# Sixteen columns of the second block's modulation moved from the MLP's up halves to two projections

## What is computed

```
mod = silu(c) @ w_ada + b_ada                   # 6 parts of 2048
sh1, sc1, gt1, sh2, sc2, gt2 = split(mod, 6)
h = rmsnorm(x, g_mix) * (1 + sc1) + sh1
x = x + gt1 * mixer(h)                          # ends in y @ w_out
h = rmsnorm(x, g_ffn) * (1 + sc2) + sh2
x = x + gt2 * ffn(h)
out = rmsnorm(x, final_g)
```

```
x = x + g1 * rmsnorm(merged @ w_o)              # the projection in front of the MLP
x = x + g2 * rmsnorm(square(relu(h @ mlp_up)) @ mlp_down)
```

## Time and profile before

| | us |
|---|---|
| median of 3 runs | 3304.55 (3303.95 to 3306.34) |
| the profiled execution | 3306.13 |
| its span, first to last instruction | 3304.4 |
| TensorE busy | 3223.1 |
| VectorE busy | 2204.1 |
| ScalarE busy | 1242.0 |
| GpSimd busy | 196.1 |
| granted TensorE clock, mean | 0.991 |

### The profile page before, as it was taken

The page is one execution under the profiler, slowest core; times in us unless marked ns, Lnnn a source line. Parts: engine busy times, 40 slices in busy tenths (PEclk is TensorE's granted clock), DMA queues, the critical chain, the costliest instruction groups (busy, mean ns, idle before and its releaser), DMA issues.

```text
span 3304.4 us, 58756 instructions
## 1 busy us (share of the span) xinstructions
PE 3223.1 (98%) x23408; PEld 2700.8 (82%) x23408; DVE 2204.1 (67%) x3396; ACT 1242.0 (38%) x1686; POOL 196.1 (6%) x298
## 2 busy tenths in 40 slices
PE   7999999999999999989999999989999999999998
PEld 4764685578888999978888888878888888888887
DVE  2377656665555666667877787787666767667666
ACT  2202130144444411344443444444544443443444
POOL 0000000012222000000000000000000000000000
PEclk9999999999999999999999999999999999999999
DMA  9956727622222688636767777645444557556654
GB/s 409 364 204 229 275 85 262 253 75 91 96 92 85 263 332 346 235 142 253 277 245 268 254 260 257 254 167 180 160 152 178 191 190 264 209 188 243 227 178 153
DMA packets 101013, 709.02 MB, mean 215 GB/s; under 512 B 11200, under 2 KB 11328, under 8 KB 19520
## 3 DMA queue, kind: packets, MB, share of 16 engines
q1 hardware_dynamic: 73872, 525.89, 43.4%
q0 software_dynamic: 23184, 169.88, 13.8%
q10 hardware_dynamic: 3744, 10.23, 0.8%
HBM read 698.36 MB, written 7.60 MB: 214 GB/s over the span
## 4 chain that ended last, share of the span: by engine, by line
PE 91%; DVE 4%; DMA 3%; issue 1%; ACT 1%; DVEq 0%; SPq 0%; POOL 0%; POOLq 0%; ACTq 0%
PE ps L2708 33%; PE ps L2707 17%; PE ps L633 11%; PE ps L2411 3%; PE ps L1100 3%; PE ps L399 2%; PE ps L2704 2%; PE ps L1823 2%; PE ps L1101 2%; PE ps L1102 2%; PE ps L1837 1%; PE ps L1092 1%; PE ps L2705 1%; PE ps L2392 1%; PE ps L2394 1%; PE ps L2393 1%
## 5 line engine op out<-in xcount | busy, mean ns | idle before, releaser
L2708 PE MATMUL ps<-hT_parts,rows_parts 128*128 128x512 f32 x3210 | 1130.2, 394 | 0.0
L2707 PE MATMUL ps<-hT_parts,ring_parts 128*128 128x256 f32 x3210 | 900.8, 281 | 2.1 <-DVE hT_parts L2680 2.1
L2671 DVE TENSOR_TENSOR ring_parts<-ring,rows_parts 128x2048 fp32r<-128x2048 f32 (+1 forms) x337 | 761.8, 2261 | 108.0 <-ACT rows_parts L2666 107.1
L2666 ACT ACTIVATE rows_parts<-ring 128x2048 fp32r<-128x2048 f32 (+1 forms) x337 | 639.3, 1897 | 407.8 <-DMA ring<-in_mlp_u 210.0
L2708 PEld LDWEIGHTS ps<-hT_parts,rows_parts 128*128 128x128 f32 x3210 | 603.0, 188 | 125.8
L2707 PEld LDWEIGHTS ps<-hT_parts,ring_parts 128*128 128x128 f32 x3210 | 607.7, 189 | 12.8 <-DVE hT_parts L2680 3.3
L2708 PE MATMUL ps<-work_parts,rows_parts 128*128 128x512 f32 x1616 | 570.1, 394 | 0.0
L2707 PE MATMUL ps<-work_parts,ring_parts 128*128 128x256 f32 x1616 | 453.7, 281 | 0.0
L633 PE MATMUL ps<-hT,ring 128*128 128x512 f32 (+1 forms) x1088 | 365.6, 498 | 0.0
L2708 PEld LDWEIGHTS ps<-work_parts,rows_parts 128*128 128x128 f32 x1616 | 303.6, 188 | 63.7
L633 PEld LDWEIGHTS ps<-hT,ring 128*128 128x128 f32 x1088 | 206.6, 190 | 157.3 <-issue 145.0
(11 more groups left out here) (495 smaller groups left out, 4481.7 us busy)
## 6 DMA issues: line engine op xcount, KB each, us to landing
ring<-in_mlp_u SPq DMA_DIRECT2D x128, 1024.0 KB, 5.0
ring<-in_ffn_u SPq DMA_DIRECT2D x88, 1024.0 KB, 4.9
rows<-in_mod_r POOLq DMA_DIRECT2D x64, 1024.0 KB, 5.3
ring<-in_gate_u SPq DMA_DIRECT2D x64, 1024.0 KB, 5.3
work<-in_ada_r POOLq DMA_DIRECT2D x64, 1024.0 KB, 5.3
ring<-in_in_u SPq DMA_DIRECT2D x36, 1024.0 KB, 4.9
rows<-in_ada_r POOLq DMA_DIRECT2D x32, 1024.0 KB, 9.3
ring<-in_down_u SPq DMA_DIRECT2D x32, 1024.0 KB, 4.9
```

The source lines that it names most:

```text
L2666: act.activation(unit_high(u)[:, 0:size], slot(u)[:, 0:size], ACT.Copy).then_inc(hi_done, 1)
L2671: dve.tensor_tensor(ring_parts[:, ring_slot(u), 0:size], slot(u)[:, 0:size], unit_high(u)[:, 0:size].bitcast(F32), ALU.subtract)\
L2707: pe.matmul(ps[:, b, low_half], low, top(kt), start=False, stop=False)
L2708: mm = pe.matmul(ps[:, b, :], high, both(kt), start=False, stop=kt == kts - 1)
```

## The change

The 16 columns of the MLP's up halves are taken out. Eight are done in `Mix`, behind units 1 and 3 of each turn of four, and eight in the output projection at the head of `Ffn2`, behind units 0 and 2 of each turn. The order of the columns stays. `Mix` gets a GpSimd part that fetches eight rows once `Merge` has split its sum; `Mlp` fetches 32 instead of 48; `Ffn2` fetches eight once the mixer's output is split, ahead of its waits and clearings. The first `late_free` and `late_done` are given at the start of `Mix` on VectorE. `gffn` moves from the start of `In2` to the last unit of the output projection, where it waits for the last of the 48 columns.

```diff
+        MIX_ROWS = OUT2_ROWS = KT // 2
@@ class Mix
+            def gpsimd(pool, own):
+                pool.wait_ge(x_split, KT)
+                fetch_late(pool, 0, MIX_ROWS)
@@ wo_sum
                             rms_y1.add_square(dve, sq1[:, bass.ds(it * 4 + j, 1), :], j, it * 4, it * 4)
+                        if j % 2:
+                            late_column(dve, it, j // 2, 2)
+                dve.sem_inc(late_free, 1)
+                dve.sem_inc(late_done, 1)
                 rms_y1.clear_sum(dve)
@@ Mlp
-        UP_COLUMNS = (2, 5, 8, 11)
-        MLP_COLUMNS = LATE_ROWS // QUARTERS
+        UP_COLUMNS = ()
+        MLP_ROWS = LATE_ROWS - MIX_ROWS - OUT2_ROWS
+        MLP_COLUMNS = MLP_ROWS // QUARTERS
                 pool.wait_ge(x_split, KT)
-                fetch_late(pool, 0, LATE_ROWS)
+                fetch_late(pool, MIX_ROWS, MLP_ROWS)
                 dve.sem_inc(act_split, 2)
-                dve.sem_inc(late_free, 1)
-                dve.sem_inc(late_done, 1)
-                dve.wait_ge(late_done, LATE_ROWS + 1)
+                dve.wait_ge(late_done, MIX_ROWS + MLP_ROWS + 1)
@@ In2
-                own.step(dve.scalar_tensor_tensor(gffn, adaT[:, 4 * KT:5 * KT], 1.0, vec("g_ffn"), ALU.add, ALU.mult))
@@ Ffn2
             def gpsimd(pool, own):
+                pool.wait_ge(x_split, 4 * KT)
+                fetch_late(pool, MIX_ROWS + MLP_ROWS, OUT2_ROWS)
                 pool.wait_ge(nadd, 3 * KT)
@@ out2_sum
                             rms_x3.add_square(dve, squared[:, j % 2, :], j, it * 4, it * 4)
+                        if j % 2 == 0:
+                            late_column(dve, it, MIX_ROWS + MLP_ROWS + j // 2, 2)
+                        elif last and j == 3:
+                            dve.wait_ge(late_done, LATE_ROWS + 1)
+                            own.step(dve.scalar_tensor_tensor(gffn, adaT[:, 4 * KT:5 * KT], 1.0, vec("g_ffn"), ALU.add, ALU.mult))
+                            own.settle()
```

More of the change, by code:

```diff
@@ L2826, in branch_kernel @@
         use_mlp = [bk.take(b, QUARTERS * MLP_USES) for b in range(MLP_BANKS)]
-        UP_COLUMNS = (2, 5, 8, 11)
-        MLP_COLUMNS = LATE_ROWS // QUARTERS
+        UP_COLUMNS = ()
+        MLP_ROWS = LATE_ROWS - MIX_ROWS - OUT2_ROWS
+        MLP_COLUMNS = MLP_ROWS // QUARTERS
+        assert MLP_COLUMNS == len(UP_COLUMNS) + KT // 2
         act_parts = work_parts[:, 0:2 * KT * T].rearrange("p (a t) -> p a t", a=KT)
@@ L2917, in vector @@
                             if n in UP_COLUMNS:
-                                late_column(dve, q, UP_COLUMNS.index(n), MLP_COLUMNS)
+                                late_column(dve, q, MIX_ROWS + UP_COLUMNS.index(n), MLP_COLUMNS)
                         else:
@@ L2924, in vector @@
                             if n % 2 == 0:
-                                late_column(dve, q, len(UP_COLUMNS) + (n - KT) // 2, MLP_COLUMNS)
+                                late_column(dve, q, MIX_ROWS + len(UP_COLUMNS) + (n - KT) // 2, MLP_COLUMNS)
                     rest_unit(dve, seg_mlp + 2 * KT + AHEAD_DVE, q * (2 * KT))
-                dve.wait_ge(late_done, LATE_ROWS + 1)
+                dve.wait_ge(late_done, MIX_ROWS + MLP_ROWS + 1)
                 rms_y2.vector(dve)
@@ L3762, in _ @@
                 Merge.gpsimd(pool, own)
+                Mix.gpsimd(pool, own)
                 Mlp.gpsimd(pool, own)
```

## The result

The changed kernel takes 3310.05 us (median of 18 runs, 3305.06 to 3315.48) where the kernel before takes 3303.88 us (median of 18, 3298.63 to 3306.34). The ratio is 1.0021, with an interval of 1.0014 to 1.0028: **slower by 6.9 us** (4.6 to 9.3; from the ratio, the two medians alone are 6.2 us apart). In a second measurement of the same two kernels the ratio was 1.0023 (1.0014 to 1.0032). The forecast was 3307.5 us, +3.0, with "no change" as the likeliest case. The time is inside the stated range; the loss is over twice what the prediction's sum gave, and just beyond the 0.2% that was called no change.

The account below looks back on a forecast made before the run. TensorE was taken to bound the kernel, so only seams could change: -2.14 + 1.08 + 2.4 + 1.66 = +3.0 us, added to the median 3304.55 for 3307.5 us. The range was 3303.5 to 3310.5 us.

Parts of the forecast that it names:

- The bound: Whole kernel: TensorE is busy 98% of the span, so freeing VectorE in the up halves gains nothing; only seams change.
- rival 4: Up halves: VectorE or transfers hold them after all, hidden by busy time; faster, 3266 us; chance 0.02.
- Seam 1: Start of the MLP: first row no longer in front of the ring transfers; gain 2.14 us, bounds 0 and 2.5.
- rival 5: Start of the MLP: the fetch does not start early and the gain is missed; 3309.6 us; chance 0.06.
- Seam 2: End of the first projection: eighth column delays the norm's reciprocal; loss +1.08 us, bounds 0.5 and 1.3.
- rival 2: TensorE's lower clock after longer idling in the norms, seams 2 and 4; at most 1.7 us, 3309.2 us; chance 0.10.
- Seam 3: Start of the second projection: first row lands behind the ring transfer, stalling unit 3; +2.4 us, bounds 0 and 3.0.
- Rival 1: Start of the second projection: row gets ahead of the ring transfer, no stall; 3305.1 us; chance 0.12.
- Seam 4: End of the second projection: eighth column behind unit 14 delays unit 15's sum; +1.66 us, bounds 1.2 and 1.8.
- Inside the second projection: Middle of the second projection: a column makes the next sum 1.7 us late, bank wanted 2.6 us later; costs nothing.
- rival 3: Second projection: two banks too few if rows land later than 10.5 us; at 12.5 us, 3321 us; chance 0.04.
- The sum: Four seams together: -2.14 + 1.08 + 2.4 + 1.66 = +3.0 us, giving 3307.5 us.

Follow-up runs that it names:

- e5: The kernel before with the two signals releasing the first row moved ahead of the first projection, no column moved; 3299.47 us, ratio 0.9992.
- e10: The kernel before, unaltered, traced a second time; one run, 3296.88 us.
- e9: The changed kernel with six columns in each projection, behind units 1 and 3, none in the last turn, four back in the up halves; 3303.58 us, ratio 1.0006.
- e6: The kernel before with the up halves' columns behind units 5, 8, 11, 14 instead of 2, 5, 8, 11; 3300.95 us, ratio 0.9998.
- e2: The changed kernel with only the second projection's eight columns; the other eight back in the up halves, ready signals in the MLP's code; 3306.75 us, ratio 1.0022.
- e1: The changed kernel with only the first projection's eight columns; the other eight back in the up halves, scale back at the input projection; 3305.44 us, ratio 1.0010.
- e3: The changed kernel with the first projection's column ahead of the square's addition instead of behind it; 3309.75 us, ratio 1.0025.
- e11: The changed kernel with six columns in each projection, none in the last turn, each ahead of the addition of the squares; 3301.21 us, ratio 0.9997.
- e7: The kernel before with the first row released early and the up halves' columns behind units 5, 8, 11 and 14; 3300.82 us, ratio 0.9997.
- e8: The changed kernel, unaltered, traced and timed once more; 3309.15 us, ratio 1.0023.
- e12: The changed kernel with the first projection's column ahead of the square's addition, measured a second time; 3306.93 us, ratio 1.0009.

## Why the prediction was right or wrong

- **The bound: right.** TensorE loses and gains nothing in the middle of the MLP and of the first projection, and in the second nothing from the second unit behind the stall on. Sixteen columns, 41.6 us of VectorE, left the up halves and bought nothing there (0.00 us between unit 7 and the last product); rival 4 is dead.
- **Seam 1: right, against the trace read.** Forecast -2.14, measured -2.17, by the mechanism named (e5). Against e10 the gain is 1.16. The bounds of 0 and 2.5 held, and rival 5 is dead; the step that failed in part is that one trace was taken for the kernel.
- **Seam 2: wrong, the largest miss.** Forecast +1.08, measured +3.58. The column in the norm was right in place and nearly in size (0.87). The failed step is "Inside this segment a column delays the next sum by about 0.9 us, against a full unit of 5.6 us until the bank is wanted; nothing." It asked only whether TensorE would have to wait for a bank inside the segment. It did not ask whether VectorE makes the delay up before the segment ends. Sums of units 10 to 12 in the kernel after, with a column between the last two:

```profile
1418.81 0.42 DVE L2755 TENSOR_TENSOR work<-work,ps 128x256 f32 x1
1423.83 0.41 DVE L2755 TENSOR_TENSOR work<-work,ps 128x256 f32 x1
...
1430.16 0.41 DVE L2755 TENSOR_TENSOR work<-work,ps 128x256 f32<-128x256 f32 x1
```

A unit without a column takes VectorE's chain 5.02 us (with the waits for ScalarE's square and rounding in it, which are part of the chain), one with a column 6.33: 11.35 us for two units. TensorE needs 2 x 5.59 = 11.18. The chain is 0.17 us too long here (the pairs before this one took 11.26 to 11.98), so it doesn't catch up. VectorE starts behind in the kernel before as well, but at 5.02 against 5.59 it gains 0.57 us a unit, and by its fourth sum it waits for ScalarE again:

```profile
1367.64 0.41 DVE L2754 TENSOR_TENSOR work<-work,ps 128x256 f32 x1
...
1383.41 0.42 DVE L2754 TENSOR_TENSOR work<-work,ps 128x256 f32 x1 [0.49 <-ACT work L2749]
```

  The lag is harmless as long as TensorE runs, and what is left of it, 2.20 us, comes due where TensorE waits for the last sum. It is not all there at the start. In the kernel before a sum that is on time starts 0.84 us behind the start of TensorE's next unit (0.61 us in the last turn). Against that the first sum of after is 1.2 us late (before's is 1.0), the one behind the first column 2.0, since VectorE waited 0.60 us for the first row, and the one at the last turn's start 3.3; the last turn, with a shorter chain, takes 1.1 off. Its rival, the hold in the norm alone, would have left e9 at 0; e9 had 1.44. The busy share of VectorE hid this (56% of the middle of this projection before the change, by the earlier trace rows, and 75% with the columns), since the waits inside the chain count as idle. The other 0.51 us are the clock, which rival 2 had as a possibility.
- **Seam 3: the stall right, what follows it missing.** Forecast +2.4, measured +3.71. The ring went first, the row landed in 7.4 us (forecast about 8.0), and the stall was 2.15 us. By the Trainium skill (DMA: Bandwidth & Descriptors, Anatomy of one DMA, SWDGE path) the row would take 4.4 us alone, an estimate; the traces don't agree: a row alone ahead of the ring took 5.3 us in e6, one beside it 7.4 here. What is missing showed as the unit behind the stall, 1.57 us at a granted clock of 0.76. Rival 2 had the clock, but priced it only at seams 2 and 4, "at most 1.7 us", and not where the change makes a stall of its own. And e2 shows that a clock that stays up would not have saved the forecast: the late row leaves VectorE behind, and 1.41 us of that come due at seam 4 instead. The step that failed is the same as at seam 2, that a late VectorE costs nothing between the seams. Rival 1 is dead: the row never got ahead.
- **Seam 4: right in its term.** The last sum is 1.47 us late, forecast 1.66. The forecast took VectorE to be on time at unit 14; in after it was, within 0.1 us at the column's start, but only behind the slow unit (e2's last sum is 2.88 us late). The stretch's total depends on the clock: it is +0.76 in e10 and +1.47 in e1, neither with a column there, so the +1.72 can't be all put down to the change; against e10 it is +0.96.
- **Inside the second projection: right for TensorE.** TensorE is busy for 56.00 of 56.00 us, and VectorE waits for no row behind the first in a way that reaches TensorE; rival 3 is dead. What the lag does up to the segment's end is told at seam 3.
- **The sum.** The four seams came to 3.58 - 2.17 + 3.71 + 1.72 = +6.84 us instead of +3.0. The misses are +2.50 at seam 2 (2.20 of lag, 0.51 of clock, less 0.21 of hold) and +1.31 at seam 3 (1.57 of clock, less 0.25 of stall). The timed difference is 6.9, but this nearness is partly luck: all stretches of the same two traces give 6.16 us, and against the second trace of before they give 7.2. That the time fell inside the stated range is luck too, since both large losses, at seams 2 and 3, were taken too small.

## What to carry to other kernels

An engine with idle time can still have no room: add up its serial chain over one period of the loop, waits for its neighbours included, and compare it with the period of the bound engine. If it is longer by anything at all, a lag that was made up before now reaches the seam, and each new delay adds to it. Put filler work into a wait that the chain has anyway (e3: ahead of the square's addition) and leave it out of a loop's last turn (e9); e11 did both, and its ratio was 0.9997. Where a change makes one transfer late, the stall is not the whole price: the engine that waited stays behind, and its debt is paid by a slow unit or at the segment's end (5.2 to 6.0 us for seams 3 and 4, where the stall is 2.15). And take a difference of under 0.3% from stretches of two traces of each kernel, not from spans.

The lowest ratio of all versions is e5's, the early row alone, at 0.9992 (0.9983 to 1.0001): not clear of no change. e7 has the same early row and came to 0.9997.

## What the runs showed of the hardware

- **The clock behind a short stall.** TensorE idled 1.98 and 1.86 us in front of one unit of after and e8, and was granted 0.76 over that unit; in e3 and e12 (1.83 and 1.91 us) the unit took 7.1 us too. Behind 1.79 us in e2 the clock stayed at 1.00. The unit cost 1.5 to 1.7 us more in 4 of 5 traces; what decides between the two cases, these traces don't show.
- **The clock in the norm.** The four spreading products at seam 2 took 1.19 to 1.20 us in all six traces with a column in front of the reciprocal (TensorE idle for 1.1 to 1.5 us there), and in two of the eight without one (e7, e10; idle 0.64 to 0.65); in the other six, 0.68. So this 0.5 us is mostly, not wholly, the change's.
- **The clock over the whole.** The mean granted clock was 0.9917 over 93 runs of the kernel before and 0.9903 over those of the kernel after and e8 (29 runs), and within one kernel the time falls as the clock rises (of before's runs, the seven at 0.990 took 3305.7 us on average, the 17 at 0.993 3299.2). The scatter of about 3 us goes with the clock, and one profile can be 6 us off its kernel (e10's 3296.88 us, where the median of its group is 3302.65).
- **Two 1 MB transfers of two queues are served mostly one after the other.** Row and ring issued together at 2454.7 landed in 7.4 and 5.8 us. Until 2458.1 all that moved, 0.70 MB, was the ring's; in the next 1.7 us both moved, 0.34 MB each; the rest was the row's. The rows of before show the same order. Being second cost a row 2.1 us (7.4 instead of the 5.3 in e6) and the ring's two transfers 2.0 to 2.5 us (the earlier trace rows against the earlier trace rows).
